# Expert layers as dense matmuls over all experts in place of gathered rows, in a two-layer streaming encoder step

## What is computed

```python
q = (xr @ w_query).reshape(n, 8, 2, 128)
s = jnp.einsum('nhcd,ckd->nhck', q, sub_keys)      # 2 x 128 key scores of each of 8 heads
s1, i1 = lax.top_k(s[:, :, 0], 16); s2, i2 = lax.top_k(s[:, :, 1], 16)
# the best 16 of the 16 x 16 sums; expert = i1 * 128 + i2, one of 16384
gate = jax.nn.softmax(top_s, axis=-1)
u = expert_u[eidx]
h = gelu(jnp.einsum('nhkd,nd->nhk', u, xr))
out = jnp.einsum('nhk,nhkd->nd', gate * h, expert_v[eidx])
```

## Time and profile before

| | |
|---|---|
| median of 3 runs | 3103.62 us |
| the profiled execution | 3110.61 us |
| its span | 3108.8 us |
| its mean granted TensorE clock | 0.832 |
| TensorE busy, share of the span | 69% |
| VectorE busy | 58% |
| GpSimd busy | 34% |
| ScalarE busy | 22% |
| moved by DMA | 1039.60 MB, 334 GB/s on the mean |

### The profile page before, as it was taken

How to read it: one execution, slowest core, us unless ns; L and a number is a source line. 1 busy time by engine, 2 the same in 40 slices (tenths; PEclk the granted TensorE clock), 3 DMA queues, 4 the chain that set the end, 5 groups by cost and what they waited for, 6 DMA issues and landing times. The chain is left out here.

```text
span 3108.8 us, 33005 instructions
## 1 busy us (share of the span) xinstructions
PE 2152.5 (69%) x11433; PEld 1141.4 (37%) x11433; DVE 1792.3 (58%) x4150; ACT 672.7 (22%) x1953; POOL 1072.5 (34%) x1022
## 2 busy tenths in 40 slices
PE   6879897566776866757668585576666767545655
PEld 3337676424443532522225232234223434322222
DVE  2364537355885664683655755747835445865554
ACT  2122111121221221121521113411212321121111
POOL 1024222333354643333433333333333223344442
PEclk9989899678888987878779698888878888877787
DMA  3440330789979899989999999999999999889997
GB/s 132 156 177 33 145 113 24 290 342 390 383 290 412 344 391 419 407 328 419 397 397 419 391 369 415 357 413 419 372 400 369 419 403 414 328 316 420 420 420 325
DMA packets 154900, 1039.60 MB, mean 334 GB/s; under 512 B 18288, under 2 KB 19488, under 8 KB 36336
## 3 DMA queue, kind: packets, MB, share of 16 engines
q0 software_dynamic: 119152, 832.67, 67.0%
q1 hardware_dynamic: 35584, 204.82, 16.7%
HBM read 1007.53 MB, written 23.63 MB: 332 GB/s over the span
## 5 line engine op out<-in xcount | busy, mean ns | idle before, releaser
L1353 POOL DMA_INDIRECT fl_pairs<-in_peer_uv,fl_row_at x652 | 738.8, 1133 | 1275.8 <-PE fl_acc L1326 1142.4
L1326 PE MATMUL fl_acc<-fl_pairs,fl_diag 128*64 128x512 f32 x2608 | 840.7, 748 | 434.0 <-ACT fl_diag L1299 413.0
L1279 DVE CUSTOM_DVE_ANT_0 fl_pairs<-fl_pairs,fl_rows 128x1024 f32<-128x1024 f32 x652 | 795.5, 1240 | 448.1 <-DMA fl_pairs<-in_peer_uv,fl_row_at 447.1
L1326 PEld LDWEIGHTS fl_acc<-fl_pairs,fl_diag 128*64 128x64 f32 x2608 | 282.2, 162 | 838.6 <-issue 779.3
L1305 ACT ACTIVATE fl_acts<-fl_dots 128x2 f32<-128x2 f32 x384 | 78.1, 203 | 1282.5 <-DVE fl_dots L1279 1282.2
L1299 ACT ACTIVATE fl_diag<-constants_sb,fl_mix 128x64 f32<-128x64 f32 x768 | 224.5, 341 | 304.5 <-DVE fl_mix L1269 302.9
L1326 PE MATMUL fl_acc<-fl_more,fl_diag 128*64 128x512 f32 x464 | 155.7, 771 | 99.0 <-ACT fl_diag L1299 99.0
L1353 POOL DMA_INDIRECT fl_more<-in_peer_uv,fl_row_at x116 | 133.2, 1148 | 219.7 <-PE fl_acc L1326 198.7
L1279 DVE CUSTOM_DVE_ANT_0 fl_more<-fl_more,fl_rows 128x1024 f32<-128x1024 f32 x116 | 140.0, 1222 | 94.2 <-DMA fl_more<-in_peer_uv,fl_row_at 94.1
L1269 DVE TENSOR_TENSOR fl_mix<-fl_row_gate,fl_acts 128x2 f32<-128x2 f32 x384 | 73.1, 192 | 133.1 <-ACT fl_acts L1305 76.8
L1684 PE MATMUL aacc<-pc_piece,at_xT 128*128 128x512 f32 x288 | 138.3, 624 | 12.1 <-PEq L1611 12.1
(11 more groups left out here) (552 smaller groups left out, 2869.5 us busy)
## 6 DMA issues: line engine op xcount, KB each, us to landing
pc_piece<-in_kvq_by_pair SPq DMA_DIRECT2D x36, 1024.0 KB, 9.4
pc_piece<-in_query_by_head SPq DMA_DIRECT2D x32, 1024.0 KB, 9.4
pc_piece<-in_past_k SPq DMA_DIRECT2D x16, 1024.0 KB, 14.6
pc_piece<-in_past_v SPq DMA_DIRECT2D x16, 1024.0 KB, 12.6
ro_w_ring<-in_rwkv_w_rkv SPq DMA_DIRECT2D x24, 512.0 KB, 8.7
ops<-operands SPq DMA_DIRECT2D x12, 1024.0 KB, 10.6
pc_piece<-in_out_by_pair SPq DMA_DIRECT2D x12, 1024.0 KB, 9.3
fl_pairs<-in_peer_uv,fl_row_at POOLq DMA_INDIRECT x652, 15.3
```

Source lines behind the costliest of these rows:

```text
L1279: dve.tensor_tensor_reduce(pair, pair, self.rows[:, u % 2, j, :], 1.0, 0.0, ALU.mult, ALU.add, self.dots[:, u % 2, q, j:j + 1]).then_inc(* ...
L1326: mm = pe.matmul(self.acc[j * FOLD:(j + 1) * FOLD, half, :], self.diag[:, self.summed % self.DIAGS, j, :], self.pair(g)[:, D + half * HALF ...
L1353: pool.indirect_dma_start(self.pair(g), None, self.io["peer_uv"], bass.IndirectOffsetOnAxis(ap=self.row_at[:, u % TILES, j, q:q + 1], axis ...
```

## The change

No row is gathered any more. Line numbers here are those of the changed kernel.

`experts` (L1332) is one stage, called once per layer for all 384 tokens. It goes over all 16384 experts in 128 blocks of 128, that is 16 chunks of 8 blocks:

- **Queries and keys** (L1547, L1494) for the three tiles at once, with a moving operand of 384 tokens.
- **dots** (L1506): 8 matmuls of 128 by 384 per block give the products of a block's 128 rows u with all tokens. ScalarE takes the gelu into `weight`.
- **The first 80 blocks** (`EARLY` = 10 chunks) have dots alone, and beside them runs the choice on VectorE (`Picks`, once per tile). The 6 chunks that don't fit into `weight` are stored to memory (`spill`) and come back later (`reload`).
- **spread**: the gates of a token over all 16384 experts are a sum over its 128 slots of a one-hot row of 128 times a one-hot column of 128. GpSimd writes one one-hot (`hot_a`, L1670), VectorE the other, times the gate (`hot_b`, L1640), one instruction per token on each. TensorE multiplies them (L1524), 4 tokens in a set, 96 sets, begun beside blocks 28, 46 and 64, with 4 sets ahead of a block. ScalarE copies the result, and issues its store to `picks` in memory, 12 parts of 2 MB.
- **rows** (L1536): VectorE multiplies a block's gelus by its gates from memory (L1650), and 6 matmuls of 128 by 512 per block add up the outputs of all tokens. For 48 blocks they stand beside the dots of the blocks that are left, then alone for 80.
- The layer norm of the three tiles ends the stage.

The tables come as pieces of 1 MB, two blocks each, through a ring of 4 places on SyncE's queue.

**All other stages stand alone**, one after another, without ticks of a flow: `time_mixing` (the three tiles in turn by `wkv_chunks`, `wkv_states` and `wkv_outputs`), `to_features`, `project_and_norm`, `mixing_weight`, the expert stage of layer 0, then `attention` (projections, two of `prompt_attention`, `sample_attention`, `head_norm`, `project_and_norm`), then the expert stage of layer 1. Their weights are loaded in the stage that uses them. `rwkv_operands` is as it was.

The core of the diff:

```diff
-            pool.indirect_dma_start(self.pair(g), None, self.io["peer_uv"],
-                                    bass.IndirectOffsetOnAxis(ap=self.row_at[:, u % TILES, j, q:q + 1], axis=0)).then_inc(...)
-                dve.tensor_tensor_reduce(pair, pair, self.rows[:, u % 2, j, :], 1.0, 0.0, ALU.mult, ALU.add,
-                                         self.dots[:, u % 2, q, j:j + 1]).then_inc(*self.dot_done.by())
-                    mm = pe.matmul(self.acc[j * FOLD:(j + 1) * FOLD, half, :], self.diag[:, self.summed % self.DIAGS, j, :],
-                                   self.pair(g)[:, D + half * HALF:D + (half + 1) * HALF],
-                                   start=(q == 0), stop=(q == TURNS - 1), tile_position=(0, j * FOLD))
+def experts(core, io, layer, xT):
+    CHUNK, CHUNKS = 8, EXPERTS // P // 8
+    EARLY, SPILLED, W_PLACES = 10, 6, 5
+    PLACES = 4
+    QUARTER, FOUR = 32, 4
+    SETS, PER_BLOCK = P // FOUR, 4
+    START = (28, 46, 64)
+    order = list(range(SPILLED, CHUNKS)) + list(range(SPILLED))
...
+                def dots(i):
+                    if i % 2 == 0:
+                        pe.wait_ge(*ready(U_PIECE[i // 2]))
+                    if i >= 2:
+                        pe.wait_ge(*d_done.at(i - 1))
...
+                    for k in range(KD):
+                        mm = pe.matmul(work[:, i % 2, 0:TOK], u[:, k, :], xT[:, k, :], start=(k == 0), stop=(k == KD - 1))
+                    mm.then_inc(*d_psum.by())
+                def spread(n):
+                    pe.wait_ge(*a_hot.at(n + 1))
+                    pe.wait_ge(*b_hot.at(n + 1))
+                    if n >= 5:
+                        pe.wait_ge(*p_done.at(n - 4))
+                    for i in range(FOUR):
+                        mm = pe.matmul(acc[:, 1 + n % 5, i * P:(i + 1) * P], hot_a[:, n % 2, i, :], hot_b[:, n % 2, i, :])
+                    mm.then_inc(*p_psum.by())
+                def rows(n, i):
+                    at = n * CHUNK + i
+                    if i % 2 == 0:
+                        pe.wait_ge(*ready(V_PIECE[at // 2]))
+                    pe.wait_ge(*weighed.at(at + 1))
+                    v = tile(V_PIECE[at // 2])[:, i % 2 * D:(i % 2 + 1) * D]
+                    for t in range(TILES):
+                        for h in range(2):
+                            mm = pe.matmul(acc[:, 2 * t + h, :], weight[:, place(n), i, t * P:(t + 1) * P], v[:, h * HALF:(h + 1) * HALF],
+                                           start=(at == 0), stop=(at == CHUNK * CHUNKS - 1))
+                    mm.then_inc(*v_psum.by())
...
+                for i in range(EARLY * CHUNK):
+                    if i + 2 in START:
+                        turn_slots(START.index(i + 2))
+                    for n in sets_ahead(i):
+                        spread(n)
+                    dots(i)
+                pe.wait_ge(*p_done.at(SETS * TILES))
+                for n in range(CHUNKS):
+                    for i in range(CHUNK):
+                        if EARLY + n < CHUNKS:
+                            dots((EARLY + n) * CHUNK + i)
+                        rows(n, i)
...
+                for t in range(TILES):
+                    pool.wait_ge(*turn_done.at(t + 1))
+                    second = slots[:, t % 2, 1]
+                    for n in range(SETS * t, SETS * (t + 1)):
+                        if n >= 2:
+                            pool.wait_ge(*p_psum.at(n - 1))
+                        for i in range(FOUR):
+                            w = n % SETS * FOUR + i
+                            ins = pool.tensor_scalar(hot_a[:, n % 2, i, :], keys, second[:, w:w + 1], None, ALU.is_equal)
+                        ins.then_inc(*a_hot.by())
```

More of the change, by code:

```diff
@@ new lines, in _ @@
+                for m in range(HC):
+                    if m % 2 == 0:
+                        pe.wait_ge(*ready(m // 2))
+                    if m >= 2:
+                        pe.wait_ge(*q_done.at(m - 1))
+                    w = tile(m // 2).rearrange("p (k n) -> p k n", k=KD)
+                    for k in range(KD):
+                        mm = pe.matmul(work[:, m % 2, 0:TOK], w[:, k, (m % 2) * P:(m % 2 + 1) * P], xT[:, k, :], start=(k == 0), stop=(k == KD - 1))
+                    mm.then_inc(*q_psum.by())
+                    if m % 4 == 0 and m > 0:
+                        key_products(m // 4 - 1)
@@ L1669, in _ @@
             def _(sp):
-                pieces.load(sp, first + 3 * KD // 2 + pieces.PLACES)
-            @block.gpsimd
-            def _(pool):
-                for n in range(1, TICKS + 1):
-                    flow.gpsimd(pool, n)
+                for n in range(3 * PAIRS):
+                    if n >= PLACES:
+                        sp.wait_ge(*w_used.at(n - PLACES + 1))
+                    sp.dma_start(ring[:, n % PLACES], io["kvq_by_pair"][n].rearrange("p a b -> p (a b)")).then_inc(*came[n % PLACES].by(16))
@@ L1677, in _ @@
+                for t in range(TILES):
+                    sp.wait_ge(*turned.at(t + 1))
+                    store(sp, 0, t)
+                    sp.wait_ge(*free.at(2 * (TILES + t) + 2))
+                    store(sp, 1, t)
+                sp.wait_ge(*stored.at(16 * 2 * TILES))
             @block.tensor
             def _(pe):
-                for n in range(3 * KD):
-                    i, k = divmod(n, KD)
-                    if n % 2 == 0:
-                        pe.wait_ge(*pieces.ready(first + n // 2))
-                    for h in range(2):
-                        mm = pe.matmul(acc[:, 2 * i + h, :], xT[:, k, :], pieces.tile(first + n // 2)[:, n % 2 * D + h * HALF:n % 2 * D + (h + 1) * HALF],
-                                       start=(k == 0), stop=(k == KD - 1))
-                    mm.then_inc(*aw_used.by())
-                    flow.tensor(pe, n + 1)
@@ L1702, in _ @@
-                copy_half(act, 2, 1)
-                flow.scalar(act, TICKS - 1)
-                flow.scalar(act, TICKS)
+                for i in range(3):
+                    for t in range(TILES):
+                        for h in range(2):
+                            act.wait_ge(*full.at(2 * (TILES * i + t) + h + 1))
+                            act.copy(tok[names[i]][:, t, h * HALF:(h + 1) * HALF], acc[:, 2 * t + h, :]).then_inc(*free.by())
             @block.vector
@@ L2199, in key_scores @@
-def key_scores(core, io, flow, pieces, xT, choice, layer, t, last, after=None, **events):
-    first = pieces.first["query0" if layer == 0 else f"query1{t}"]
-    with ExitStack() as ctx:
-        part = LateScores(core, io, flow, ctx, pieces, first, xT, choice, layer, f"late{layer}{t}")
-        flow.plan(part.ticks, last, lags=flow.LOOSE, **events)
-        with core.nc.Block(no_gpsimd_drain=True) as block:
-            @block.sync
-            def _(sp):
-                part.loads(sp)
-                if after is not None:
-                    after(sp)
-            @block.gpsimd
-            def _(pool):
-                for n in range(1, flow.ticks + 1):
-                    flow.gpsimd(pool, n)
-            @block.tensor
-            def _(pe):
-                part.products(pe)
-            @block.scalar
-            def _(act):
-                part.copies(act)
-            @block.vector
-            def _(dve):
-                part.best(dve)
-        core.end_stage()
@@ new lines, in program @@
+        with ExitStack() as rwkv:
+            gated = rwkv.enter_context(nc.sbuf_tensor("gated_wkv", [P, TILES, D], F32))
+            time_mixing(core, io, gated)
+            mixT = rwkv.enter_context(nc.sbuf_tensor("mixT", [P, KD, TOK], F32))
+            to_features(core, gated, mixT, "rwkv", TILES)
+            project_and_norm(core, io, mixT, io["mix_by_pair"], 0, "rwkv", TILES)
+        mixing_weight(core, io, neg_lam)
+        for layer in range(2):
+            if layer == 1:
+                attention(core, io, neg_lam)
+            with ExitStack() as mixer:
+                xT = mixer.enter_context(nc.sbuf_tensor(f"ex_xT_{layer}", [P, KD, TOK], F32))
+                to_features(core, core.x_tok, xT, f"ex_{layer}", TILES)
+                experts(core, io, layer, xT)
```

2032 lines of the change are left out of this document (562 added, 1470 removed).

## The result

The changed kernel takes **4472.59 us** (median of 4 runs, 4470.77 to 4476.01); the kernel before took 3106.64 us beside it (4 runs, 3101.92 to 3115.83). The ratio is 1.439 [1.436, 1.443]: 44% slower. The forecast was 4,410 us, so the time lies 1.4% above it and inside the range. The profiled execution took 4476.01 us, with a span of 4474.2.

What follows compares the result with a forecast made beforehand. TensorE's dense expert matmuls were to replace the DMA stream as the limit: 3,144 us for both expert stages plus 1,268 us for all others gave a 4,412 us span, forecast as 4,410 us, range 4,300 to 4,560 us.

Steps and rivals of the forecast that it cites:

- Which resource takes over: Whole kernel: transfers stop being the limit; TensorE's dense expert matmuls take 3,016 us for both layers.
- The price of a record and their number: Expert matmuls: each fp32 matmul is two records, 0.430 us for 512 columns, 0.323 for 384, 0.12 for 128.
- The wait for GpSimd: Spread: at 0.30 us per GpSimd one-hot, TensorE stands some 1.0 us per block, 24 us a layer.
- One-hots in turn at the port: Spread: GpSimd's and VectorE's one-hots exclude each other, 58 us more, 4,470 us; chance 0.12.
- The choice beside the dots: Expert stage: VectorE's choice, 34 us per tile, is hidden under nine blocks of dots, 46 us.
- Layer norms of the stage: End of each expert stage: three layer norms, a table load and the last product, 23 us.
- Query part: Expert stage, per layer: queries 83 us and keys 12 us on TensorE, some handshakes, first piece's load 9 us.
- The stages outside: All stages outside the two expert layers, now bare of the gather stream: 1,268 us in sum.
- Prompt attention: Attention layer: tile 0 between 30 and 50 us, taken as 40, and 46 for tile 1, 86 us together.
- Sample attention: Attention layer: between 94 and 146 us, taken as 120 and 8 to begin, 128 us.
- stage ends: Outside the expert layers: 0.3 to 0.5 us for some 28 stages, and the last store, 17 us.
- Faster, or the clock gone for good: Dense matmuls: two records overlap, 2,902 us, chance 0.02; or granted clock falls to 0.832, 5,020 us, chance 0.03.

Runs made afterwards that it cites:

- e6: Changed kernel with dots over half the features and rows giving half the outputs, first block of rows kept whole: 3152.46 us.
- e7: Changed kernel with each of the 256 expert table pieces loaded a second time into an unread spare tile: 4472.98 us.
- e8: Changed kernel with four one-hot buffers, one of GpSimd's four one-hots per set on VectorE, and dots and rows in bfloat16, converted by ScalarE: 2621.56 us.
- e5: Changed kernel with four one-hot buffers in place of two, and one of GpSimd's four one-hots per set written by VectorE: 4225.58 us.
- e3: Changed kernel with four buffers of one-hots in place of two on both engines: 4249.18 us.
- e4: Changed kernel with VectorE writing only one of its four one-hots per set after the first two sets: 4475.94 us.
- e2: Changed kernel with one of GpSimd's four one-hots per set written by VectorE, still two buffers: 4383.63 us.
- e1: Changed kernel with the spread over 48 blocks of dots, two sets each, in place of 24 blocks with four: 4270.43 us.

## Why the prediction was right, and which terms were not

**Which resource takes over: right.** Gathers bounded the kernel before, dense products bound this one. e6 takes half of the products and gets back 1,320 us; e7 doubles the loads for nothing.

**The price of a record and their number: right, and this decided the case.** L1506 has 4,096 records and L1536 3,072, as counted. Dots come every 0.323 us (28 blocks of 16 in 144.84 us), rows every (5.31 - 0.59) / 11 = 0.429. That both halves of a float32 matmul cost time is shown from the other side by e8: one record, a quarter of the time. The spread's records take 0.112 us and not 0.12, which is 6 us a stage.

**The wait for GpSimd: the failed step.** "I take 0.30 us, nearest the copy", for a one-hot, with a far bound of 0.5. It takes 0.59, outside the bounds. Neither row behind them is a comparison with a value per partition, and no row gives the fixed part from which the 0.5 was made; VectorE's half, taken from such another row too, takes 0.29 and not 0.15. "TensorE stands some 1.0 us per block": a block loses 4.9 us, 24 x 4.9 = 118 us a stage and not 24, and the wait for `ex_hot_a` alone, which the prediction named as a sign, is 72.6 us a stage and not 24. The mechanism was the one described, with 0.59 put in: the third set needs 2.36 us from the end of the first, in which TensorE has 0.89 us of work, so it stands about 1.5, and again for the fourth (seen: 1.69 and 1.16). By the prediction's own sum 0.59 gives some 3.3 us a block, 79 us a stage. The sum missed a second part: when TensorE stands, the granted clock falls, and the work behind the wait is dearer. 0.92 us in the fourth set and 0.73 in the dots are a third of the 4.9. The forecast had 1.00 for all of the stage. e5 wins both parts back, and e3 nearly.

**One-hots in turn at the port (first rival, 0.12): not seen.** The 4,470 us that it gave is nearly the time measured, but for another reason. GpSimd's one-hots take 0.59 us beside VectorE's (990.25) and as long with a quarter of them (e4). What does hold GpSimd up is VectorE's operation with two inputs in SBUF. In the timelines of the changed kernel, GpSimd, VectorE and TensorE:

```profile
1096.60 6.89 POOL L1670 TENSOR_SCALAR ex_hot_a<-constants_sb,ex_slots 128x128 f32<-128x128 f32 x8 [4.18 <-PE ex_acc L1524]
```
```profile
1099.09 2.27 DVE L1302 TENSOR_TENSOR ex_scores<-pk_best 128x2048 f32<-128x2048 f32 x1
```
```profile
1103.54 2.08 PE L1524 MATMUL ex_acc<-ex_hot_b,ex_hot_a 128*128 128x128 f32 x8 [3.30 <-POOL ex_hot_a L1670]
```

Eight one-hots take 6.89 us and not 4.74, and TensorE waits 3.30 us and not 1.16. It happens where a choice begins while the last one-hots of the tokens before are written, twice a stage, some 2 us each. The Trainium skill ("SBUF — State Buffer", "Who interferes with whom") names both kinds of contention, `tensor_scalar` in the two-port modes and two inputs in SBUF. With the second the trace agrees, by the 6.89 us above; the first, with `tensor_scalar`, no run here shows for these one-hots, whose compared values come from a column per partition.

**The choice beside the dots: right.** TensorE never waits for it in the changed kernel. ScalarE's gelus and copies took 4.5 us in a block with spread (35.96 in eight) and not under 3, and stayed hidden. How near it was shows e8, where a block of dots takes 2.6 us: 13 us of waits for the second and the third choice.

**Layer norms of the stage:** 21 us against 23. **Query part:** 96.7 us, against 83 + 12 and some handshakes; the first piece was waited for 5.9 us and not 9.

**The stages outside: 1,168 us, not 1,268.** The two errors cancel in part: the expert stages took 2 x 82 us more, the rest 100 less, which the prediction itself had named as a sign of being wrong. That the time lies in the range is luck to this extent: with the 1,268 us as forecast, the two stages of 1,654 us would have given a span of 4,576 us, above the range's end of 4,560. The start (234 against 233) and `attention_projections` (135 against 136) were right, the recurrence with its outputs and the last states came to 447 against 458. Two were far too dear. Prompt attention and the change to the sample part took 62 us (71.2 less two `to_features`) where 86 stood, and the first prompt alone 24, below the "between 30 and 50" of the forecast. That lower bound took only the flow's 20.3 us on TensorE off. In the same 50 us of the kernel before (1496 to 1546), the flow also held VectorE for 23 us (19 dot products, L1279), and ScalarE loaded the table that its function needs 16 times, in turn for the prompt (L1800) and for the flow's gelu (L1305):

```profile
L1800 ACT ACT_TABLE_LOAD x8 | 10.3, 1283 | 1.1 <-PEq L1611 1.0
L1305 ACT ACT_TABLE_LOAD x8 | 10.3, 1283 | 0.1
```

These 20.6 us of loads are one of 1.28 us in the changed kernel's first prompt. How much each part had cost, no run separates. Sample attention took 104 us against 128, between its bounds. `head_norm` and the projection behind it took 91 us against 102, from 2721.4 to 2812.5. Each `to_features` takes 4 to 6 us and not 7. The 17 us for stage ends no run prices; I take them to be largely in the other terms already.

**Faster, or the clock gone for good: no.** The dense stretches have 1.00 for 548 us on end.

## What to carry to other kernels

Before replacing gathers by dense work, count the matmuls of float32 twice and set them against the whole stream: here 7,168 records cost some 2,640 us (4,096 x 0.323 + 3,072 x 0.430), more than the gathers' 2,100, and half of that price (e6) only draws level, while a quarter of it, in bfloat16, wins. A helper engine whose rate is sufficient on the mean still stalls the main one if its buffers let it work only while it is waited for (e2, 7.1 us of work in blocks of 8.74 and 47.7 us of waits a stage): compare its time for what is needed in one burst with what the buffers hold. Stretches that were hidden under a stream can't be priced by subtracting the stream's matmuls alone; here they came out shorter.

## What the runs showed of the hardware

- GpSimd's comparison of 128x128 against a value per partition takes 0.59 us from start to start, twice VectorE's 0.29, whatever VectorE does beside it in `tensor_scalar` (e4, 625 ns in the mean against 623).
- Waits cost more than their own length: over blocks with waits of 1.69 and 1.16 us the granted clock was 0.86 (0.50 behind the second wait), over the same matmuls without waits 1.00 (e1, e5), and the matmuls behind the waits took 1.65 us more a block.
- An operation of VectorE with two inputs in SBUF (2.27 us) beside eight such comparisons of GpSimd's made them take 6.89 us in place of 4.74.
- ScalarE loads the table for another function in 1.28 us, and where the exponential of the prompt and the flow's gelu took turns it was loaded each time: 16 loads in 50 us of the kernel before.
- ScalarE's conversion of 128x2048 from float32 to bfloat16 takes 1.90 us, 484 us in all. Not all of it stayed beside other work: in e8 TensorE waited 54.9 us for converted pieces and 68.7 us for gelus, and ScalarE itself 220 us for the loads; no run separates these.
- The kernel's own loads ran at 127 GB/s beside TensorE and at 414 when asked to (e8), and TensorE's records kept their length under doubled loads (592 and 593 ns for rows in the changed kernel and e7).
